# Merge projections of a two-block transformer kernel as three split passes, with its modulation sums moved by place

## The reference, cut to what matters

```python
for l in range(2):
    mod = silu(c) @ ada_w[l] + ada_b[l]            # 1 x 3072: a matrix times one vector
    shift, scale, gate = split(mod, 3)
    h = rms_norm(x, pre_norm[l]) * (1 + scale) + shift
    p = split_proj(h @ w_in[l])                    # ret, dsa, idx, gla parts and merge (3072 wide)
    ret, dsa, gl = three attention branches, each times silu(its gate)
    g = sigmoid(p["merge"]).reshape(B, S, 3, D)
    y = g[:, :, 0] * (ret @ w_br_ret[l]) + g[:, :, 1] * (dsa @ w_br_dsa[l]) + g[:, :, 2] * (gl @ w_br_gla[l])
    x = x + gate * rms_norm(y @ w_out[l], post_norm[l])
```

## Time and profile before

| | us |
|---|---|
| runs, median of 3 | 1189.54 (1189.35 to 1190.0) |
| profiled execution, whole | 1190.94 |
| profiled execution, span | 1189.0 |
| PE busy in the span | 1104.8 |
| DVE busy | 640.3 |
| ACT busy | 402.3 |
| POOL busy | 101.2 |

### The profile page before, as it was taken

How to read it: one execution, slowest core, us unless ns; L and a number is a source line. 1 busy time by engine, 2 the same in 40 slices (tenths; PEclk the granted TensorE clock), 3 DMA queues, 4 the chain that set the end, 5 groups by cost and what they waited for, 6 DMA issues and landing times.

```text
span 1189.0 us, 12378 instructions
## 1 busy us (share of the span) xinstructions
PE 1104.8 (93%) x4700; PEld 712.3 (60%) x4700; DVE 640.3 (54%) x1279; ACT 402.3 (34%) x848; POOL 101.2 (9%) x115
## 2 busy tenths in 40 slices
PE   1699999999997999999999979999988998998997
PEld 1487775554444877756544468855566457346773
DVE  7529766453324397677833261255678564235642
ACT  0436546330024365463300262343343013215431
POOL 3205010000000051100000001300000000230000
PEclk9999999999998999999999989999987999999999
DMA  7634532577323444316664243112051025332000
GB/s 324 241 135 185 210 136 80 212 282 282 143 67 132 164 174 183 142 71 225 271 272 152 83 169 142 71 71 114 28 230 71 1 93 202 134 141 90 1 1 35
DMA packets 14026, 171.21 MB, mean 144 GB/s; under 512 B 1792, under 2 KB 2048, under 8 KB 3344
## 3 DMA queue, kind: packets, MB, share of 16 engines
q1 hardware_dynamic: 12800, 167.65, 37.1%
q10 hardware_dynamic: 1168, 2.77, 0.6%
HBM read 169.37 MB, written 1.05 MB: 143 GB/s over the span
## 4 chain that ended last, share of the span: by engine, by line
PE 79%; DVE 11%; ACT 5%; DMA 2%; POOL 1%; issue 1%; ACTq 0%; DVEq 0%
PE bank L646 18%; PE bank L946 15%; PE bank L668 10%; PE bank L912 7%; PE bank L987 6%; PE bank L638 4%; DVE wlo L1815 3%; PE bank L1160 2%; PE bank L1176 2%; PE bank L719 2%; PE bank L630 2%; DVE ekd L1762 1%; PE bank L1118 1%; PE bank L1021 1%; PE bank L802 1%
## 5 line engine op out<-in xcount | busy, mean ns | idle before, releaser
L646 PE MATMUL bank<-ring,hT 128*128 128x512 f32 (+1 forms) x576 | 244.4, 580 | 0.5 <-DVE hT L1805 0.4
L946 PE MATMUL bank<-ring,hT 128*128 128x512 f32 (+2 forms) x544 | 199.3, 526 | 2.3 <-ACT eqT L1225 1.4
L646 PEld LDWEIGHTS bank<-ring,hT 128*128 128x128 f32 x576 | 108.5, 192 | 119.7 <-issue 114.1
L946 PEld LDWEIGHTS bank<-ring,hT 128*128 128x128 f32 x544 | 100.4, 194 | 91.6 <-issue 88.4
L1815 DVE TENSOR_TENSOR wlo<-ring,whi 128x512 fp32r<-128x512 f32 x120 | 89.8, 773 | 45.5 <-ACT whi L1253 45.3
L668 PE MATMUL bank<-whi,xhi 128*128 128x512 f32 (+1 forms) x256 | 99.4, 388 | 6.3 <-DVE wlo L1815 4.4
L668 PE MATMUL bank<-whi,xlo 128*128 128x512 f32 (+1 forms) x256 | 97.0, 379 | 0.0
L668 PE MATMUL bank<-wlo,xhi 128*128 128x512 f32 (+1 forms) x256 | 96.7, 378 | 0.0
L1253 ACT ACTIVATE whi<-ring 128x512 fp32r<-128x512 f32 x120 | 72.6, 628 | 65.3 <-PE bank L668 65.2
L668 PEld LDWEIGHTS bank<-whi,xhi 128*128 128x128 f32 x256 | 48.0, 187 | 21.9 <-issue 7.9
L1762 DVE SCALAR_TENSOR_TENSOR retqkv<-ring,cnow,retqkv 128x512 f32<-128x512 f32 x84 | 58.5, 749 | 1.0
(11 more groups left out here) (381 smaller groups left out, 1695.8 us busy)
## 6 DMA issues: line engine op xcount, KB each, us to landing
ring<-in_weights SPq DMA_DIRECT2D x73, 2048.0 KB, 8.8
ring<-in_weights SPq DMA_DIRECT2D x5, 1024.0 KB, 5.3
ring<-in_weights SPq DMA_DIRECT2D x2, 1360.0 KB, 6.3
ring<-in_weights SPq DMA_DIRECT2D x1, 1536.0 KB, 8.6
kk<-in_k SPq DMA_DIRECT2D x1, 1120.0 KB, 8.4
X<-in_x ACTq DMA_DIRECT2D x1, 1024.0 KB, 16.6
kc<-in_k ACTq DMA_DIRECT2D x1, 1024.0 KB, 10.9
X<-in_context SPq DMA_DIRECT2D x1, 1024.0 KB, 7.5
```

What stands on the lines that cost most here:

```text
L646: mm = pe.matmul(ps[:, 0:width], hT[:, k, t * P:(t + 1) * P], ring[:, slot, k * stride + w0:k * stride + w0 + width], start=(k == 0), stop ...
L946: mm = pe.matmul(ps[:, 0:width], hT2[:, k, t * P:(t + 1) * P], ring[:, slot, k * width:(k + 1) * width], start=(k == 0), stop=(k == KD - 1))
```

## The change

- `PIECES1` also holds the six merges (48 more pieces in a layer, 108 in all). Their steps use `project_split`. ACT makes all high parts. Of the merge pieces every second one (`POOLED`, odd i) gets its low part from GpSimd (`low_pool`), the others from DVE. ACT copies both halves of a merge out at its second step.
- A ring slot of a merge is free when its last two lows are made, not when PE has multiplied.
- `ada_rows` on PE takes the place of `mod_sum` where `summed_on_pe` says so, and everywhere in the prologue and the even layer: 8 float32 matmuls with 32 weight columns (three condition vectors, the rest zero), the four of a round writing four different strips of 32 partitions of a bank. ACT copies the result out (`ada_out`), and `ada_columns` picks and adds (8 records, 16 columns wide). In the first layer all six sums stay on DVE; in the second layer m 0 to 3 go to PE and m 4, 5 stay; in the odd layer both stay.
- Prologue: SP loads `col` ahead of the ring, with the positions and frequencies in it; ACT issues ident and x at once; x is normalised and turned beside the modulation chunks.
- `COLUMNS_AT`: the `ada` of m 0 to 3 moves to g 10, 12, 14, 16. DVE gates the first half of dsa at g 8. ACT's Sigmoid over `G` is shorter. `hT`, `L`, `PT`, `retT`, `dsaT` have other places, and `yT` is its own tile.

```diff
 PIECES1 = [... ("ret_g", 512), ("dsa_g", 512), ("gla_g", 512)) + MERGE_WIDTHS
+def summed_on_pe(l, m):
+    return l == DEPTH - 1 and m < SHIFTS
+        POOLED = [q for q, (name, i, _) in enumerate(PIECES1) if name.startswith("merge") and i % 2]
...
+            sp.dma_start(col[:], cols).then_inc(event("col_in"), 16)
             for c in range(RING):
                 load(c, c, CH0[c][1])
             for c in range(RING, len(CH0)):
-                sp.wait_ge(event("ada_sum"), c - RING + 1)
+                filled(sp, pro, f"s_ada{c - RING}")
...
                     elif CH1[c - RING][0] in SPLIT1:
-                        sp.wait_ge(event("lo1_ready"), l * len(PIECES1) + SPLIT1[CH1[c - RING][0]])
+                        last = SPLIT1[CH1[c - RING][0]] - 1
+                        low_ready(sp, last, l)
+                        if last in POOLED:
+                            low_ready(sp, last - 1, l)
+                    elif CH1[c - RING][0].startswith("ada") and not summed_on_pe(l, int(CH1[c - RING][0][3])):
+                        sp.wait_ge(event("ada_sum"), sum_number(l, int(CH1[c - RING][0][3])))
...
+            def ada_rows(u, name, slot):
+                ps = begin(u, "s_" + name)
+                for k in range(KD):
+                    g = k % 4
+                    mm = pe.matmul(ps[GROUP * g:GROUP * (g + 1), :], cst[:, k, :], ring[:, slot, k * 512:(k + 1) * 512],
+                                   start=(k < 4), stop=(k >= 4))
+                done(u, "s_" + name, mm)
+            def ada_columns(u, name, rows, picks):
+                ps = begin(u, name)
+                for j in range(4):
+                    mm = pe.matmul(ps[:, j * PICK:(j + 1) * PICK], rows[:, j * P:(j + 1) * P], picks, start=True, stop=True)
+                done(u, name, mm)
...
                     for t in range(TT):
-                        if name in SPLIT1:
-                            project_split(name, l, t)
-                        else:
-                            project(u, f"{name}{t}", slot, t, 512, l)
+                        project_split(name, l, t)
                         gap(g)
+                        if g in COLUMNS_AT:
+                            ada1(l, COLUMNS_AT[g])
                         g += 1
-                    if name.startswith("merge") and name != "merge0":
-                        m = int(name[5]) - 1
-                        ada(u, f"ada{m}", msum[:, m % 2], conds(l, m), l * MERGES + (SHIFTS + m + 1), l)
+                    if name.startswith("merge") and summed_on_pe(l, int(name[5])):
+                        ada_rows(u, f"ada{name[5]}", landed(f"ada{name[5]}"))
...
+                def low_pool(first, last):
+                    for q in range(first, last):
+                        if q in POOLED:
+                            pool.wait_ge(event("hi1_ready"), l * len(PIECES1) + (q + 1))
+                            pool.tensor_tensor(wlo1[:, q % BUFFERS, :], piece1(q)[2], whi1[:, q % BUFFERS, :],
+                                               ALU.subtract).then_inc(event("lo1_pool"), 1)
...
-                        if name in SPLIT1:
-                            low(40 + 4 * g, min(44 + 4 * g, len(PIECES1)))
+                        low(40 + 4 * g, min(44 + 4 * g, len(PIECES1)))
...
                     if name.startswith("merge"):
                         m = int(name[5])
-                        mod_sum(CH1, [n for n, _ in CH1].index(f"ada{m}"), len(CH0), msum[:, m % 2], conds(l, m),
-                                cact if own else cnow, l)
+                        if not summed_on_pe(l, m):
+                            c = [n for n, _ in CH1].index(f"ada{m}")
+                            arrived(dve, CH1, c, len(CH0), l)
+                            mod_sum((len(CH0) + c) % RING, msum[m % 2], conds(l, m)[0])
...
-E_SUM = {0: ("adag4", range(KD)), 5: ("adag5", range(KD)), 6: ("ada0", range(KD))}
+E_SUMS = {1: "adag4", 5: "adag5", 6: "ada0", 9: "ada1", 11: "ada2"}
```

More of the change, by code:

```diff
@@ L469, in conds, with sum_number, e_rows @@
         def conds(l, m):
-            return 2 if l == DEPTH - 1 and m < SHIFTS else 1
-        def sum_number(c):
-            return SHIFTS + DEPTH * MERGES + sum(name.startswith("ada") for name, _ in CH2[:c + 1])
+            return (1, 2) if l == DEPTH - 1 and m < SHIFTS else (0, 1)
+        PLAIN = [(l, m) for l in range(DEPTH) for m in range(MERGES) if not summed_on_pe(l, m)]
+        SUMS1 = len(PLAIN)
+        def sum_number(l, m):
+            return PLAIN.index((l, m)) + 1
         def chunk2(name):
             return [n for n, _ in CH2].index(name)
+        E_ROWS = [name for name, _ in CHE if name.startswith("ada")]
+        def e_rows(name):
+            return msum2[E_ROWS.index(name) % 2]
         SPLIT1 = {name: q + 1 for q, (name, _, _) in enumerate(PIECES1)}
@@ L619, in done, with ada, ada_summed, ada1 @@
                 ins.then_inc(bank_full[u.at[name][0]], 1)
-            def ada(u, name, sums, vectors, count, rep=0):
-                pe.wait_ge(event("ada_sum"), count)
-                ps = begin(u, name, rep)
-                for j in range(4):
-                    for v in range(vectors):
-                        at = 64 * (vectors * j + v)
-                        mm = pe.matmul(ps[:, at:at + 64], sums[:, v, j * P:(j + 1) * P], ones[:, 0:64],
-                                       start=True, stop=True)
-                done(u, name, mm)
+            def ada_rows(u, name, slot):
[10 more added lines that the diff above has]
+                done(u, name, mm)
+            def ada(u, name, rows):
+                emptied(pe, u, "s_" + name)
+                ada_columns(u, name, rows, sel)
+            def ada_summed(u, name, rows, count):
+                pe.wait_ge(event("ada_sum"), count)
+                ada_columns(u, name, rows, ones[:, 0:PICK])
+            def ada1(l, m):
+                if summed_on_pe(l, m):
+                    ada(lay1[l], f"ada{m}", msum[m % 2])
+                else:
+                    ada_summed(lay1[l], f"ada{m}", msum[m % 2], sum_number(l, m))
             def turn_blocks(ps, blocks):
@@ L1749, in mod_sum, with mod_out @@
-            def mod_sum(chunks, c, chunks_before, sums, vectors, cond, rep=0, rows=range(KD)):
-                if rows[0] == 0:
-                    arrived(dve, chunks, c, chunks_before, rep)
-                slot = ring[:, (chunks_before + c) % RING, :]
-                for k in rows:
-                    for v in range(vectors):
-                        w = slot[:, k * 512:(k + 1) * 512]
-                        if k == 0:
-                            ins = dve.tensor_scalar(sums[:, v, :], w, cond[:, k, v:v + 1], None, ALU.mult)
-                        else:
-                            dve.wait_ge(event("dve_step"), steps[0] - vectors + 1)
-                            ins = dve.scalar_tensor_tensor(sums[:, v, :], w, cond[:, k, v:v + 1], sums[:, v, :],
-                                                           ALU.mult, ALU.add)
-                        if k == KD - 1 and v == vectors - 1:
+            def mod_out(u, name, m, which, picked):
+                ps = filled(dve, u, name)
+                v, n = picked
+                dve.tensor_tensor(mod[:, 4 * m:4 * m + 4, 0:n],
+                                  ps[:, 0:4 * PICK].rearrange("p (j c) -> p j c", j=4)[:, :, v:v + n],
+                                  adab[:, which, 4 * m:4 * m + 4].unsqueeze(2).broadcast_to([P, 4, n]),
+                                  ALU.add).then_inc(free(u, name), 1)
@@ L1765, in mod_sum @@
+            def mod_sum(slot, rows, v):
+                for k in range(KD):
+                    w = ring[:, slot, k * 512:(k + 1) * 512]
+                    if k == 0:
+                        step(dve.tensor_scalar(rows, w, cst[:, k, v:v + 1], None, ALU.mult))
+                    else:
+                        settle()
+                        ins = dve.scalar_tensor_tensor(rows, w, cst[:, k, v:v + 1], rows, ALU.mult, ALU.add)
+                        if k == KD - 1:
                             ins.then_inc(event("ada_sum"), 1)
@@ L1959, in head_norm, with gated @@
                     gated(o, st[:, at + 24:at + 32], 4, gate, ready, silu)
[L1961 removed]
+                def gated(o, factor, heads, gate, ready, silu, rows=range(TT)):
                     dve.wait_ge(event("silu_ready"), l * 3 + silu)
[L1963 removed]
+                    for t in rows:
                         settle()
[L1965 removed]
+                        ps = filled(dve, u, f"{o}{t}")
                         w = 512 // heads
```

589 lines of the change are left out of this document (306 added, 283 removed).

## The result

The change makes the kernel slower: 1201.0 us (median of four runs, 1197.7 to 1202.0) against 1189.8 for the kernel before on the same chip, ratio 1.0092 with a 95% interval of 1.0073 to 1.0111. The forecast was 1197.5, with slower as the likelier side. The profiled execution has a span of 1199.9 us where that of before had 1189.0.

The account below looks back on a forecast made before the run. PE bounds the layers, a serial DVE job the prologue, both the even layer. Prologue -12, first layer +24, second +4, even -7, rest -1 make +8 on 1189.5: 1197.5 us; own range 1187 to 1210, with rivals 1155 to 1220.

Parts of the forecast that it names:

- A merge step: Merges on PE: a split step takes 5.76 us where a plain one takes 6.92, 1.16 less for each of 24.
- Prologue, -12: Start to idx: no serial DVE work left, loads set the end, 12 us less (bounds -9 and -15).
- First layer, +24: First layer's merges: load, pieces and sum in series outlast PE's work, 24 us more (bounds +7 and above +28).
- the circle: First layer: load, high, low and DVE sum follow each other for each merge, 20.9 us where PE needs 12.4.
- the hold: DVE stands still during GpSimd instructions, in the third piece's low and in the sum: 3.7 us a merge.
- Step 7: Both layers: PE waits some 7 us for ACT's high parts, then loses about 1.5 us at half pace.
- Second layer, +4: Second layer: shorter steps and ada against rows, the wait before step 7 and br0's later load, 4 us more.
- Even layer, -7: Even layer: waits -8, half pace -9, narrower ada -5.4, six ada_rows +15, together 7 us less.
- Rest, -1: Odd layer: `cnow` copies and narrower columns, 1 us less; memory plan and earlier dsa half at nothing.
- B: Rival, chance 0.22: GpSimd doesn't hold the sum in the first layer, which is then +10; 1181.5 us in all.
- C: Rival, chance 0.13: the ring's circle doesn't bind, loads and sum lie beside other work; 1165.5 us.
- D: Rival, chance 0.14: the strips don't overlap, ten ada_rows cost 4.4 us more each, the prologue 9; 1250 us.

Follow-up runs that it names:

- e1_pe_sums: The kernel after, with the sums of ada0 to ada3 on TensorE in the first layer as well: 1188.5 us, ratio to before 0.9982.
- e3_all_dve: The kernel after, with all low parts of the merges on DVE and none on GpSimd: 1194.5 us, ratio to before 1.0043.
- e5: The kernel after, with ACT making step 7's high parts before the head sums and Silu, DVE's retention norm ending iteration 6: 1196.1 us.
- e11: The kernel after, with all six sums on TensorE, ACT's squares in iteration 4, root and Silu in iteration 6 behind the copies: 1182.6 us.
- e9_plain_merges: The kernel after, with plain float32 merges that read only the high part of the rows: 1177.7 us, ratio to before 0.9894.
- e4: The kernel after, with the eight matmuls of an ada_rows accumulated in one strip instead of four: 1261.0 us, ratio to before 1.0609.
- e12: The kernel after, with plain float32 merges from the whole x, gates laid over parts no longer needed: 1178.8 us, ratio to before 0.9907.

## Why the prediction was right, point by point

**A merge step.** 5.76 against 6.92 us: the warm steps of after have 5.67 to 5.72. Right.

**Prologue, -12.** -11.3. An ada_rows was put at 2.5 us warm and is 1.85. The Trainium skill, "TensorE: Matmul & The Clock Gate", section "Part 3: Packing small matmuls — row/col tiling", has 2.38 times for three strips, from which 2.9 us was estimated. The run with one strip gives 3.8 times for four.

**First layer, +24.** +19.0. The mechanism is the one given: the circle over load, highs, low, sum, load. e1_pe_sums removes it and 14.1 us with it; e3_all_dve shortens a turn to 17.2 to 17.7 us where the prediction gave 17.1 without the hold. The five sums were to end at 203.5, 227.1, 248.0, 268.9 and 289.8 (the prediction's times less the prologue's 12); the loads behind them start at 206.4, 226.1, 245.7, 265.9 and 286.2. So the first turn was put 4 us too long (19.7 against 23.6), and the mis-sized term is the hold, taken at 3.7: it was 0.7, in the one low (1.40), and the sum itself ran unheld (0.48 + 5.48). The two DSA units took 2.6 of their 2.8, the load 8.0 of 8.6. The later turns, 19.6 to 20.3, are near the 20.9. The hold in the last two of them is as it was taken, 2.9 us in the sum (1.50 + 7.39 against 5.96) and 0.7 in the low before it, 3.6 against 3.7, and 2.6 in the one ahead of these. What is shorter is the load (8.2 and 8.3) and the highs (1.68 for 1.89). (The working adds 17.1 + 3.7 up to 20.9; it is 20.8.) Of the 19.0 us 2.0 are not the circle's: idx takes 11.71 us where it had 9.68, on a PE that has waited. The Trainium skill, "SBUF — State Buffer", section "SBUF: two separate sides", has the lock taken for a whole instruction, which was estimated to give 22 us a turn; the measured turns, 20.3 at most, are below that. A held instruction took 1.67 to 1.80 us where a free one has 0.76, about 1.0 more, and KL of the same shape on GpSimd takes 1.28 alone; so the hold exists, for most of the other's instruction.

**Step 7.** 7 us of wait and 1.5 of half pace: 6.91 and, in the second layer, 7.41 for a step of 5.7. Right. What no part of the prediction says, and e5 and e11 showed, is that neither of two other orders passes the block: each time the next one behind it waited.

**Second layer, +4.** -1.5. Four ada_rows at 1.85 instead of 2.5 are 2.6 us of it, and the other 3 are br0's load. sum(4) was to end 238.9 us behind idx (285.5 less 46.6) and ended at 234.1 (613.12 less 379.06); br0's load then ran beside PE's step 17 (7.35 us), and br0 starts at 621.17 with no PE wait for it beyond 0.04 us. What was put down as a loss of 3 us was none.

**Even layer, -7.** +1.7, the step that failed in the profiled execution. It had four terms: 8 us of waits, 9 of half pace, 5.4 for narrower columns, and 15 for rows. Between 776 and 927 us before, PE was idle 9.8 us; in the same part of after (783 to 936) 4.6, so 5 of the 8 came. The 9 us of half pace didn't: a granted clock of 0.93 before and 0.93 after, over the same 138 to 140 us. The prediction said that what is late next is ACT, "hardly less than PE's"; it was, two waits of 1.4 us, with the half pace behind them. Yet the same instructions with the same waits took 131.5 us in e5_step7 and in e9_plain_merges, at a mean clock of 0.99: 6.5 less than before, close to the -7 (the rows, 6 x 1.85 = 11.1 for 15, make up for the 3 us of waits that stayed). So the edit can give what was forecast, and in after it did not; which of the two comes is open. It was wrong to count half pace as a fixed amount that goes with its waits in proportion.

**Rest, -1.** +3.0: 0.7 between the layers, 0.3 ahead of e_g0 and 2.0 behind e_o0, where one load in the chain takes 9.5 us instead of 8.4 and PE waits 1.8 us for it instead of 0.7.

**The sum and the rivals.** +8 was forecast, +10.9 measured in the profiled executions. The size is near because errors cancel: the layers were put 10.5 us too high, and the even layer and the rest 12 too low. B (no hold) is out by the held sums in after and their lengths in e3, C (the circle doesn't bind) by e1, D by e4. That the split merges cost the first layer its time is the finding that the runs support best: 14 us by e1, 9 by e3, 19 by e9 and e12.

## What to carry to other kernels

Before an operation is given new feeder work on other engines, draw the circle that closes through the ring of buffers: load, feeders, the last reader that frees the slot, load. If it is longer than the operation that was made faster, the gain is lost however much room the busy shares show; the cure is to take one member out of the circle (the sum to TensorE, or no feeders), not to reorder it, which here gained nothing.

Judge stages, not the total: the even layer, in which ten of the kernels do not differ, moved their times by up to 8 us. With two pauses of 1.4 us in a stretch of light matmuls it took 131.5 us in two kernels and 136.4 to 139.7 in eight. Halving the pauses brought nothing (139.6), and the one version without them has 129.9. It is worth trying to remove such a wait wholly, but one profile does not tell a cure from a lucky execution.

## What the runs showed of the hardware that I had not expected

- Four column strips of 32, float32 in 128x512, run 3.8 times as fast as the same eight matmuls in one strip (1.85 against 6.98 us for 16 records).
- A scalar_tensor_tensor with two SBUF inputs on DVE takes 1.67 to 1.80 us instead of 0.76 when a GpSimd tensor_tensor is on, and the tensor_scalar ahead of it, with a single input, 1.30 to 1.50 instead of 0.48. From 170 to 300 us, 23 lows on GpSimd (35.0 us of its time) spared DVE nothing: DVE has 66.5 us for its 22 lows and the sums (38.3, 22.3 and 5.9), where in e3_all_dve 44 lows and the same sums take 62.3 (31.6, 27.8 and 2.9).
- The same instructions with the same waits took 131.5, 136.4, 138 or 139.7 us in the even layer, at a mean granted clock of 0.99 to 0.93. With the two waits for the gate rows taken out it was 129.9, in one profile. Behind the same pause of 1.4 us the clock was 0.60 over ten us in after and 0.93 in e9_plain_merges. What in the timing of the pauses decides is open: no run placed them on purpose.
